# Two feed-forward phases with paired hidden halves, and 512-column projections in the latent mixers

## What is computed

```python
x = x + 0.5 * swiglu(rms_norm(x, g0), w_gate, w_up, w_down)       # 1024 -> 2816 -> 1024
x = x + mixer(rms_norm(x, g1))
x = x + 0.5 * swiglu(rms_norm(x, g2), w_gate2, w_up2, w_down2)

def swiglu(h, w_gate, w_up, w_down):
    return (silu(h @ w_gate) * (h @ w_up)) @ w_down
```

## Time and profile before

| | us |
|---|---|
| median of 3 runs | 2416.87 (2415.67 to 2416.99) |
| the profiled execution | 2416.62 |
| its span, first to last instruction | 2414.8 |
| TensorE busy | 2390.3 (99%) |
| VectorE busy | 1782.2 (74%) |
| ScalarE busy | 1131.0 (47%) |
| GpSimd busy | 74.7 (3%) |
| mean granted clock of TensorE | 0.998 |

### The profile page before, as it was taken

How to read it: one execution, slowest core, us unless ns; L and a number is a source line. 1 busy time by engine, 2 the same in 40 slices (tenths; PEclk the granted TensorE clock), 3 DMA queues, 4 the chain that set the end, 5 groups by cost and what they waited for, 6 DMA issues and landing times.

```text
span 2414.8 us, 39931 instructions
## 1 busy us (share of the span) xinstructions
PE 2390.3 (99%) x16752; PEld 2204.8 (91%) x16752; DVE 1782.2 (74%) x2186; ACT 1131.0 (47%) x1317; POOL 74.7 (3%) x106
## 2 busy tenths in 40 slices
PE   8999999999999999999999999999999999999999
PEld 7999899999899978999999988999989999898998
DVE  8778846877877878778776766587787777666876
ACT  5335664433433664334335754433343367544432
POOL 2000000000000000100000000001000000000000
PEclk9999999999999999999999999999999999999999
DMA  6555445555555426655554534456556555344554
GB/s 215 185 182 174 131 132 191 177 190 189 177 192 184 144 70 195 207 190 177 190 190 144 175 107 138 161 189 212 189 177 191 183 159 167 105 140 157 188 180 137
DMA packets 308139, 409.43 MB, mean 170 GB/s; under 512 B 9798, under 2 KB 274464, under 8 KB 308000
## 3 DMA queue, kind: packets, MB, share of 16 engines
q1 hardware_dynamic: 304736, 401.66, 51.8%
q0 software_dynamic: 3072, 5.69, 0.8%
q10 hardware_dynamic: 192, 0.08, 0.0%
HBM read 406.35 MB, written 1.05 MB: 169 GB/s over the span
## 4 chain that ended last, share of the span: by engine, by line
PE 94%; DVE 4%; ACT 1%; issue 1%; DMA 0%; ACTq 0%; DVEq 0%
PE acc L641 25%; PE bank L579 24%; PE bank L1048 16%; PE bank L582 13%; PE acc L2362 2%; PE acc L579 1%; PE bank L605 1%; DVE part_lo L487 1%; PE bank L2886 1%; PE bank L1046 1%; PE bank L598 1%; PE acc L2379 1%; PE acc L2480 1%; DVE conv L1551 1%; PE acc L582 1%; PE bank L2334 1%
## 5 line engine op out<-in xcount | busy, mean ns | idle before, releaser
L480 ACT ACTIVATE part_hi<-raw 128x2048 fp32r<-128x2048 f32 (+1 forms) x382 | 726.9, 1906 | 919.0 <-DMA raw<-in_ffn_w 383.0
L487 DVE TENSOR_TENSOR part_lo<-raw,part_hi 128x2048 fp32r<-128x2048 f32 (+1 forms) x382 | 868.1, 2277 | 235.9 <-ACT part_hi L480 232.6
L579 PE MATMUL bank<-hT,part_hi 128*128 128x512 f32 x2560 | 641.6, 392 | 0.0
L579 PEld LDWEIGHTS bank<-hT,part_hi 128*128 128x128 f32 x2560 | 460.9, 189 | 82.9
L641 PE MATMUL acc<-gated,part_hi 128*128 128x256 f32 x2816 | 519.9, 283 | 0.0
L641 PEld LDWEIGHTS acc<-gated,part_hi 128*128 128x128 f32 x2816 | 445.1, 192 | 0.0
L1048 PE MATMUL bank<-part_hi,hT 128*128 128x256 f32 (+1 forms) x2336 | 437.5, 286 | 0.2
L641 PE MATMUL acc<-gated,part_lo 128*128 128x256 f32 x1408 | 398.5, 283 | 0.0
L1048 PEld LDWEIGHTS bank<-part_hi,hT 128*128 128x128 f32 x2336 | 370.3, 193 | 6.5 <-issue 4.7
L582 PEld LDWEIGHTS bank<-hT,part_lo 128*128 128x128 f32 x2560 | 349.2, 190 | 24.9
L582 PE MATMUL bank<-hT,part_lo 128*128 128x256 f32 x2560 | 356.9, 282 | 0.0
(11 more groups left out here) (470 smaller groups left out, 2207.1 us busy)
## 6 DMA issues: line engine op xcount, KB each, us to landing
raw<-in_ffn_w SPq DMA_DIRECT2D x132, 1024.0 KB, 5.2
raw<-in_w_in SPq DMA_DIRECT2D x52, 1024.0 KB, 5.3
raw<-in_ffn_w_up SPq DMA_DIRECT2D x44, 1024.0 KB, 5.3
raw<-in_ffn_w_down SPq DMA_DIRECT2D x44, 1024.0 KB, 4.9
raw<-in_ffn_w_gate SPq DMA_DIRECT2D x43, 1024.0 KB, 5.3
raw<-in_hy_w_in SPq DMA_DIRECT2D x22, 1024.0 KB, 5.2
raw<-in_hy_w_out SPq DMA_DIRECT2D x8, 1024.0 KB, 4.9
raw<-in_w_out SPq DMA_DIRECT2D x8, 1024.0 KB, 4.9
```

Source lines behind the costliest of these rows:

```text
L480: t.e.activation(part_hi[:, n % SLOTS, 0:size], raw[:, n % SLOTS, 0:size], ACT.Copy).then_inc(hi_ready, 1)
L487: t.e.tensor_tensor(part_lo[:, n % SLOTS, 0:size], raw[:, n % SLOTS, 0:size], part_hi[:, n % SLOTS, 0:size].bitcast(F32), ALU.subtract).th ...
L579: pe.matmul(b.rearrange("p (h s) -> p h s", h=2), slot_cols(s, 0)[:, k, f * P:(f + 1) * P], hT[:, :, k, :], start=(k == 0), stop=False, sk ...
```

## The change

**Feed-forward in two phases.** The chunks' gate and up pieces come first, 22 of them, then the down projection in 12 pieces: four blocks of 256 output columns, each in three pieces over the hidden width (8, 8 and 6 slices of 128). The hidden activations stay in SBUF in full (`ff`, high and low), and a down unit is now one 512-column matmul on both parts and one 256-column matmul, as in gate and up. The chunks use `bank` and `acc` in turn. ScalarE copies the low half of each PSUM pair out, VectorE adds the high half to it, then scales, on 512 columns instead of 1024; the high part of the product is copied by ScalarE. The root row is spread after the second gate piece. In the down phase each block is added to `xT`, and its slices of `hT` and squares are made, while the next block runs; the last piece signals its first output tile early. The output transposes are placed between the down pieces of the last feed-forward. The loops over chunks are written out.

**Openings.** The first piece takes slices 0 to 5 (feed-forward) or 0 to 6 (projection) for both tiles before the last ones.

**Latent mixers.** The first 608 columns needed are three pieces of 3, 3 and 2 slices with matmuls of 304 columns in four banks. The rest is pairs: 512 columns in two pieces of four slices, one bank for each token half. Two heads' values are made together, alternating between the column halves of the array, one step later, into all of `acc[:, 3]`, and split in one go. The decay products stand at steps 6 and 8.

The core of the diff:

```diff
-Z_TILES = (12, 13, 14, 0, 1, 2, 3, 10, 11, 4, 5, 6, 7, 8, 9)
-Z_W = [min(COLS, Z_IN - i * COLS) for i in Z_TILES]
+WIDE = 512
+Z_HALF = (Z_IN - Z_GL) // 2
+Z_FIRST_KS = ((0, 3), (3, 6), (6, KD))
...
-FFN_PIECES = [SLOT] * (3 * CHUNKS)
+FFN_UP = 2 * CHUNKS
+FFN_PIECES = [SLOT] * FFN_UP + [COLS * (k1 - k0) for _ in range(4) for k0, k1 in DOWN_KS]
 MIXER_PIECES = [[SLOT] * (6 + 4 + 12 + 8), [KD * w for w in SA_W] + [SLOT] * 4]
-MIXER_PIECES += [[KD * w for w in Z_W[0:6]] + [2 * MLA_H * MLA_QK, SLOT] + [KD * w for w in Z_W[6:]]
+MIXER_PIECES += [[(k1 - k0) * 2 * Z_HALF for k0, k1 in Z_FIRST_KS] + [SLOT] * 2 + [2 * MLA_H * MLA_QK] + [SLOT] * 11
...
+            for c in range(1, CHUNKS):
+                load_cols(t, wg, COLS * c)
+                load_cols(t, wu, COLS * c)
+            down = wd.rearrange("(k p) c -> p k c", p=P)
+            for b in range(4):
+                for k0, k1 in DOWN_KS:
+                    load(t, down[:, k0:k1, b * COLS:(b + 1) * COLS])
...
+        def down_banks(b):
+
+            return (acc, bank, bank, acc)[b][:, (0, 0, 2, 2)[b]:(2, 2, 4, 4)[b], :]
...
-                narrow(range(0, 6))
-                both(range(0, 4))
-                narrow(range(6, KD))
-                mm = both(range(4, KD))
+                narrow(f, range(0, KD - 2))
+                both(f, range(0, KD - 2))
+            for k in (KD - 2, KD - 1):
+                for f in range(2):
+                    narrow(f, (k,))
+                for f in range(2):
+                    mm = both(f, (k,))
             mm.then_inc(piece_done, 1)
...
-        def ffn_down(pe, c, s, first=False, last=False):
-            for d in range(KD):
-                for f in range(2):
-                    mm = down_tile(pe, lambda w: slot_rows(s, w)[:, f, :],
-                                   lambda g: gated[:, g, c % 2, f * S:(f + 1) * S], d, first and f == 0, last and f == 1)
-                if last and d in (1, 3, 5):
-                    mm.then_inc(acc_full, 1)
+        def ffn_down(t, k, b, s, ks, on_first=None):
+
+            pe = t.e
+            for f in range(2):
+                out = down_banks(b)[:, f, :]
+                for i in ks:
+                    pe.matmul(out.rearrange("p (h s) -> p h s", h=2), slot_cols(s, 0)[:, i - ks.start, f * P:(f + 1) * P],
+                              ff[:, :, i, :], start=(i == 0), stop=False, skip_group_check=True)
+                for i in ks:
+                    mm = pe.matmul(out[:, 0:S], slot_cols(s, 1)[:, i - ks.start, f * P:(f + 1) * P], ff[:, 0, i, :],
+                                   start=False, stop=(i == FF_K - 1), skip_group_check=True)
+                if on_first and f == 0:
+                    on_first(mm)
             mm.then_inc(piece_done, 1)
...
+                    if c == 1 and which == 1:
+                        pe.wait_ge(up_out, done + 1)
+                        if k == 0:
+                            flip_gains_tensor(t)
+                        root_row_tensor(t, bank[:, 3, :])
+                    if c > 1:
+                        pe.wait_ge(up_out if which else gate_out, done + c - 1)
+                    if c == 2 and which == 1:
+                        pe.wait_ge(root_row_ready, t.roots)
+                    ffn_up(t, c, s, which)
+
+            last_of_acc, last_of_bank = done + CHUNKS - 1, done + CHUNKS
+            room = ((gate_out, last_of_acc), (gate_out, last_of_bank), (up_out, last_of_bank), (up_out, last_of_acc))
+            for b in range(4):
+                for j, (k0, k1) in enumerate(DOWN_KS):
+                    s = arrived(t)
+                    if j == 0:
+                        pe.wait_ge(*room[b])
+                    if b == 0:
+                        pe.wait_ge(gated_ready, done + (k1 + 1) // 2)
+                    split_end = b == 3 and j == len(DOWN_KS) - 1
+                    ffn_down(t, k, b, s, range(k0, k1), (lambda mm: mm.then_inc(first_full, 1)) if split_end else None)
+                    if k == 7 and b and j == 0:
+                        out_flip_tensor(t, b - 1)
+
+        def out_flip_tensor(t, b):
+
...
+            for c in range(CHUNKS):
+                n = CHUNKS * k + c
+                v = silu_gate[:, c % 2, :]
+                act.wait_ge(piece_done, SLOTS + p + 2 * c + 1)
+                if c:
+                    act.wait_ge(gate_out, n)
+                else:
+                    act.wait_ge(sums_ready, 3 * (k // 2) + 2 * (k % 2) + 1)
+                act.activation(low_rows[:, 0, :, :], low_of(up_banks(c, 0)), ACT.Copy).then_inc(gate_low, 1)
+                next_hi(t)
+                if c:
+                    act.wait_ge(gate_scaled, n + 1)
+                    act.activation(v, v, ACT.Silu).then_inc(silu_ready, 1)
+                act.wait_ge(piece_done, SLOTS + p + 2 * c + 2)
+                if c:
+                    act.wait_ge(up_out, n)
+                act.activation(low_rows[:, 1, :, :], low_of(up_banks(c, 1)), ACT.Copy).then_inc(up_low, 1)
+                next_hi(t)
                 if c == 0:
                     t.see(root_col_ready)
+                    act.wait_ge(root_row_full, t.see(root_row_full))
                     if k == 0:
-                        act.wait_ge(root_row_full, 1)
-                        act.activation(gain[:, N_GF:N_GA + N_GB], acc[:, 1, S + N_GF:S + N_GA + N_GB], ACT.Copy)
-                    root_row_scalar(t)
-                act.wait_ge(gate_scaled, later(CHUNKS * k + c + 1, i, 4))
-                v = silu_gate[:, c % 2, :]
-                act.activation(v, v, ACT.Silu).then_inc(silu_ready, 1)
-                split_hi(t, n + LEAD + 1, i)
-                if c:
-                    split_hi(t, n + LEAD + 2, i)
-
-            chunk(0, n0)
-            chunk(1, n0 + 2)
-            if k == 0:
...
+                dve.wait_ge(gate_low, n + 1)
+                dve.tensor_tensor(v, high_of(up_banks(c, 0)), low_rows[:, 0, :, :], ALU.add).then_inc(gate_out, 1)
                 if c == 0:
-                    root_col_vector(t)
-                    split_lo(t, n + LEAD)
+                    next_lo(t)
...
+            def added(k0, k1, sig):
+                v, f0, f1 = xT[:, k0:k1, :], k0 % 2, k0 % 2 + k1 - k0
+                dve.wait_ge(down_low, t.see(down_low))
+                dve.scalar_tensor_tensor(v, high_of(down_banks(b))[:, f0:f1, :], 0.5, v, ALU.mult, ALU.add)\
+                    .then_inc(down_added, 1)
+                dve.wait_ge(down_added, t.see(down_added))
+                dve.scalar_tensor_tensor(v, down_rows[:, f0:f1, :], 0.5, v, ALU.mult, ALU.add).then_inc(sig, 1)
+                dve.wait_ge(sig, t.see(sig))
...
+        def pair_tensor(t, pair, g):
+
+            pe = t.e
+            s = arrived(t)
+            for a in range(TT):
+                for k in range(4):
+                    for p, q in PASSES:
+                        mm = pe.matmul(bank_of(pair[a]), hT[:, p, 4 * g + k, a * P:(a + 1) * P],
+                                       slot_part(s, q, 4, WIDE)[:, k, :], start=(g == 0 and k == 0 and p + q == 0),
+                                       stop=(g == 1 and k == 3 and p == 1))
+                if g and a == 0:
+                    mm.then_inc(full[pair[0]], 1)
+            mm.then_inc(piece_done, 1)
...
+                if i >= 4 and i % 2 == 0:
+                    h0 = i - 4
+                    pe.wait_ge(na_flipped, base + h0 + 2)
+                    if h0:
+                        pe.wait_ge(na_lo, pairs + h0 // 2)
+                    for st in range(TT):
+                        for h in (h0, h0 + 1):
+                            r = lo(h)
+                            mm = pe.matmul(acc[r:r + 64, 3, 0:S], z[:, st, Z_NV + h * 64:Z_NV + (h + 1) * 64],
+                                           soft_pT[:, h % 2, st * S:(st + 1) * S], start=(st == 0), stop=(st == TT - 1),
+                                           skip_group_check=True)
+                    mm.then_inc(na_value, 1)
...
+            first = [claim(t, by_piece=(j == 3)) for j in range(4)]
+            for n, (k0, k1) in enumerate(Z_FIRST_KS):
+                s = arrived(t)
+                for j, b in enumerate(first):
+                    a, c = j // 2, j % 2 * Z_HALF
+                    for k in range(k0, k1):
+                        for p, q in PASSES:
+                            if j == 0:
+                                (low_k if p else hi_k)(k)
+                            mm = pe.matmul(bank[:, b, 0:Z_HALF], hT[:, p, k, a * P:(a + 1) * P],
+                                           slot_part(s, q, k1 - k0, 2 * Z_HALF)[:, k - k0, c:c + Z_HALF],
+                                           start=(k == 0 and p + q == 0), stop=(k == KD - 1 and p == 1))
+                    if k1 == KD and j < 3:
+                        mm.then_inc(full[b], 1)
+                    if n == 1 and j == 1:
+                        root_col_tensor(t, acc[:, 0, :])
+                mm.then_inc(piece_done, 1)
+            t.see(root_col_ready)
```

(4 more changed lines are left out.)

761 lines of the change are left out of this document (429 added, 332 removed).

## The result

The changed kernel takes 2396.49 us (median of four runs, 2396.08 to 2396.88) where the kernel before takes 2416.44: ratio 0.9916, 95% interval 0.9904 to 0.9927. It is faster by 20 us, not by the 45 of the forecast, and outside the range.

A forecast was written before the change was run, and what follows sets the result against it. The prediction took TensorE, working 99% of the span, as the bound. Terms of 53.6 us saved and 7.8 lost, 45.8 net off the 2414.8 span, gave a forecast of 2371.0 us, range 2361 to 2392.

The forecast's parts named there:

- point 8: New waits: neighbourhood heads' end 4.8 us lost, other reordered latent mixer waits 2 lost (bounds 0 and 20), tail 0.5 lost.
- the latent mixers wait: Rival: latent mixers wait for banks claimed in pairs, 5 to 14 us each, total 2380 to 2400; chance 0.16.
- Point 5: Openings of feed-forwards and three mixers: more matmuls cover the wait for the last hT slices, 5.7 us saved.
- points 5 and 6: Openings, 5.7 us saved (0.4 a mixer); small ones, fewer root row matmuls and alternating GLA outputs, 1.9 saved.
- Point 1: Down projection in pairs: 1408 units go from 0.360 to 0.349 us each, 15.0 us saved.
- Point 2: Latent projections in 512 columns, the rest in 304: 10.2 us saved a mixer, 20.4 for two (bounds 12 to 24).
- Point 4: Paired values of neighbourhood heads run side by side on column halves: 3.8 us a mixer, 7.7 saved.
- Point 7: New feed-forward order on VectorE and ScalarE: nothing charged, except 0.5 us lost in the first feed-forward.
- The tail: Kernel's end: one add of 0.69 us becomes a copy and two adds of 0.48, 0.5 us lost.
- Point 3: Clock stretch at 0.50 in the first latent mixer's 96-column tile goes with that tile: 2.9 us saved.
- a rival: Less gain from pairing: values not side by side, dearer 304 columns, or clock falls in waits; 2380 to 2392, chance 0.07.

The follow-up runs named there:

- r14_all_late_claim: Changed kernel with low halves moved later, gate piece in thirds, other bank turns, later gate copies, and each pair's second bank claimed before its 13th matmul: 2366.23 us.
- r7_down_apart: Changed kernel with the 512-column matmul of each down-projection unit made as two of 256 columns: 2407.44 us.
- r1_split_behind: Changed kernel with VectorE's low half (next_lo) moved behind the neighbourhood query and key flip copies in the latent mixers: 2382.07 us.
- r4_values_apart: Changed kernel with the values of two neighbourhood heads computed one head after the other, not alternating: 2395.62 us.
- r13_late_claim: Changed kernel with the second bank of each pair claimed only ahead of the pair's 13th matmul, not with the first bank: 2385.82 us.

## Why the prediction missed

**What failed is the last term of point 8**, "other waits that I can't see in the reordered latent mixer": 2 us lost for two mixers, with bounds 0 and 20. Idle time beyond before came to 11 us a mixer, 22 in all, of which the neighbourhood heads' end has 3.6. So the term was 18 to 19 and not 2, near its upper bound. With the orders and the claim repaired (`r14_all_late_claim`) the idle time is 2.2 and 2.5 us a mixer. It wasn't invisible: the order of `next_lo` and `flip_out` stands in the diff, ScalarE's split stands behind its flip copies, and the split durations are in the earlier trace rows. I walked VectorE's order in the up phase and at the heads, and not there. The rival "the latent mixers wait" had the price right, 2380 to 2400, at a chance of 0.16; what I held against it (the chain of before shows nothing but TensorE) says nothing about an order that has changed.

**Point 5 failed for the mixers.** The feed-forward openings gained: 4.67 a pair less 3.75 of the down phase is 0.46 each, where I had 0.65. The mixer openings had a wait of 0.2 to 0.3 us to lose each, and not 0.4. The latent ones lost it; the hybrid's went from 0.28 to 0.96 and the sparse one's from 0.22 to 1.31: I had taken slice 6 as early, and again a low half stood ahead of it. With the repair the hybrid and sparse mixers took 213.93 and 110.86 (`r14_all_late_claim`), 1.1 and 0.8 less than before; 0.8 is what points 5 and 6 have for one mixer.

**The work terms were right.** Point 1: 15.0, confirmed by `r7_down_apart` (352 x 0.0106 a pair). Point 2: by starts, the projections of the second latent mixer fell from 157.5 to about 147 (without the wait of 1.7 us among them and the slow stretch), some 10 against 10.2, and the 304-column matmuls came 0.140 apart. Its lower bound was added up wrongly: with 304 columns at 21.9 us a mixer it would have been 3 and not 12. Point 4: 32 value instructions took 7.98 a mixer before and 4.06 after, 3.9 against 3.8. Point 7: no wait in the up phase. Point 8's waits at the heads: 0.94 + 0.85 against 1.4 + 1.0. The tail lost 0.7 against 0.5 (the last feed-forward gained 1.3, the first of a pair 2.0): what stands behind the last down matmul became 0.55 shorter, but 12 of the 16 output transposes moved between the down pieces, where they take 1.1 of TensorE. Of the 0.5 charged to the first feed-forward nothing shows: it is 2.6 shorter, where point 1 has 1.9.

**Point 3 was right for its place and wrong for the sum.** No profile of a kernel with the 304-column tiles has a stretch at 0.50 in that place; two of before's form have one in the first latent mixer and one also in the second. (In the earlier trace rows the granted clock is the third last figure of the window, 0.50.) But new stretches came with the new waits, and they cost more than the 2.9. TensorE is busy 267.05 and 267.89 us in the changed kernel's latent mixers and 265.59 and 265.81 in those of `r1_split_behind`, which have no stretch: together 3.5 us. The two in the hybrid and sparse mixers cost 2.9 (below). The prediction had such stretches only in a rival, at 3 us each and a chance of 0.07.

In sum, the 25.8 us between the forecast and the measured change of the span lie, by stages, about 21 in the latent mixers, 4 in the hybrid and sparse ones and 0.8 in the feed-forwards. The 21 are 15.4 of idle time beyond the 6.8 that point 8 charged, the 3.5 of the slow clock, and some 2 for the ends of the matmuls ahead of the waits, which count as busy (0.16 at the longest wait: 5.33 by starts, 5.17 idle). The 4 are 0.8 not gained and 3.2 lost. Profiles without the stretches have 215.07 for the hybrid mixer (`r4_values_apart`) and 111.95 for the sparse one (`r1_split_behind`), so the clock has 1.4 to 1.5 in each, 2.9 together; the longer waits at the openings (0.7 and 1.1) are partly made up by gains elsewhere. The 0.8 are 1.3 of feed-forward openings and 0.2 of the tail, less what the first feed-forward did better.

## What to carry to other kernels

When a change reorders an in-order engine, look for each copy that empties a buffer and list what now stands ahead of it; a background task such as a split or a prefetch may stand there only if what it waits for is earlier than the copy's own input. A larger unit (two banks at once) turns a late release that was covered into a wait: claim each buffer where it is first written. And a gain in work is to be checked by stages, busy beside idle, since a total hides both.

## What was not expected of the hardware

- **Clock stretches follow waits.** Eight of the profiled kernels have the 5.3 us wait in both latent mixers, and behind or inside each of the sixteen waits the granted clock falls to 0.50 (the 1.2 GHz level) for 3.4 or 6.8 us. With the wait at 2.5 us (`r13_late_claim`) it is one of two, without it none of eight. The window of the changed kernel (granted clock third last):

```profile
1364.10:1367.50 3.40, 3.21 (x8) 2.57 (x9) 3.40 (x5) 0.68 (x1) 0.00 (x0) 0.50 0.00 0
```

  In it 512-column matmuls start 0.43 apart and not 0.23. That the wait causes the stretch is likely by this count, but it wasn't tried apart from the wait. Why the same stretches come and go in the hybrid and sparse mixers, where code and waits are the same, stays open. Over whole runs the mean granted clock says little: the changed kernel took 2396.61 at 0.995 and 2396.08 at 0.998.

- **Two column halves of the array need no alternation.** Eight instructions of 128 rows by 64 columns for two heads take 1.01 us alternating and 1.02 one head after the other; four of one head alone take as long (1.01).

- **"issue" can be a bank.** The longest wait was put down to "issue" and not to the copy that ended it, probably because the waits for the two banks are separate instructions ahead of the matmul, which no run tried apart; with the claim apart from the first bank's (`r13_late_claim`) the profile names VectorE's copy.
